# First norm and linear attention outputs of a decoder step: scaling in place and turning by the identity, instead of multiplying by a diagonal

## What is computed

```python
def rms_norm(x, w):
    y = x * rsqrt(mean(x * x, axis=-1) + EPS)
    return y * w

h = rms_norm(x, norm_mix_pre)               # x is (1024 + 8, 1024)
z = h @ w_in                                # projection to GLA q, k, v, r and NSA q, kv, gates
o, S = gla_chunked(q, k, v, g, s0)          # 4 heads of 128 output columns
o = o * rsqrt(mean(o * o, axis=-1) + EPS) * gla_norm
y_gla = o * silu(r)
y_nsa = compressed, selected and window attention, weighted by gates
x = x + rms_norm(concat(y_gla, y_nsa) @ w_out, norm_mix_post)
x = x + rms_norm(relu(rms_norm(x, norm_ffn_pre) @ w_ff_up)**2 @ w_ff_down, norm_ffn_post)
```

## Time and profile before

| | |
|---|---|
| median of three runs | 1752.52 us |
| the profiled execution, its time | 1760.71 us |
| its span in the trace | 1758.9 us |
| TensorE busy | 1684.2 us (96%) |
| VectorE busy | 1093.2 us (62%) |
| ScalarE busy | 518.2 us (29%) |
| GpSimd busy | 830.2 us (47%) |
| mean granted TensorE clock | 0.978 |

### The profile page before, as it was taken

How to read it: one execution, slowest core, us unless ns; L and a number is a source line. 1 busy time by engine, 2 the same in 40 slices (tenths; PEclk the granted TensorE clock), 3 DMA queues, 4 the chain that set the end, 5 groups by cost and what they waited for, 6 DMA issues and landing times.

```text
span 1758.9 us, 24643 instructions
## 1 busy us (share of the span) xinstructions
PE 1684.2 (96%) x9310; PEld 1369.3 (78%) x9310; DVE 1093.2 (62%) x2113; ACT 518.2 (29%) x1100; POOL 830.2 (47%) x644
## 2 busy tenths in 40 slices
PE   8999999897999989999999989999999999999997
PEld 7888888784555557777778878888888888888886
DVE  5332111446776667776641068896789678967897
ACT  3311111337887762334222162100120012001202
POOL 3211221314454452413222189957685668476933
PEclk9999999988999999999999999999999999999999
DMA  5488893838434545646643541121021201211005
GB/s 154 138 256 255 237 278 93 247 98 268 158 126 126 175 132 216 252 161 231 223 154 108 173 170 59 50 71 59 14 72 48 72 7 66 69 52 46 3 1 193
DMA packets 172396, 233.53 MB, mean 133 GB/s; under 512 B 22488, under 2 KB 137096, under 8 KB 168120
## 3 DMA queue, kind: packets, MB, share of 16 engines
q1 hardware_dynamic: 162024, 181.64, 33.6%
q0 software_dynamic: 9216, 50.34, 8.0%
q10 hardware_dynamic: 1040, 0.00, 0.0%
HBM read 217.58 MB, written 102.45 MB: 182 GB/s over the span
## 4 chain that ended last, share of the span: by engine, by line
PE 65%; DVE 6%; issue 2%; ACT 2%; POOL 2%; another core or an unknown queue 0%; DVEq 0%
PE PS L3137 36%; PE PS L2217 7%; PE PS L2415 6%; PE PS L1870 4%; PE PS L1855 4%; PE PS L1883 4%; DVE Z L2597 1%; DVE Z L3197 1%; POOL X L3071 1%; DVE Z L437 1%; PE PS L412 1%; POOL Z L1710 1%; PE PS L506 1%; PE PS L2261 0%; DVE Z L3157 0%
## 5 line engine op out<-in xcount | busy, mean ns | idle before, releaser
L3197 DVE TENSOR_TENSOR Z<-PS,Z 128x516 f32<-128x516 f32 x432 | 288.4, 686 | 118.8 <-PE PS L3137 117.5
L2217 PE MATMUL PS<-Z 128*128 128x256 f32 x768 | 189.4, 396 | 4.1 <-issue 3.2
L2217 PEld LDWEIGHTS PS<-Z 128*128 128x128 f32 x768 | 144.1, 196 | 33.4 <-issue 13.5
L3137 PE MATMUL PS<-Z,X 128*128 128x258 f32 x584 | 138.6, 384 | 2.6 <-POOL X L3071 2.6
L3137 PE MATMUL PS<-srow,misc 128*128 128x258 f32 x560 | 133.4, 381 | 0.0
L3137 PEld LDWEIGHTS PS<-Z,X 128*128 128x128 f32 x584 | 111.7, 192 | 19.9 <-POOL X L3071 3.0
L1144 DVE TENSOR_TENSOR Z<-PS,Z 128x516 f32<-128x516 f32 x27 | 18.8, 696 | 161.1 <-PE PS L312 161.1
L3137 PEld LDWEIGHTS PS<-srow,misc 128*128 128x128 f32 x560 | 106.0, 190 | 15.8
L3137 PE MATMUL PS<-srow,X 128*128 128x258 f32 x480 | 113.3, 380 | 0.0
L270 POOL TENSOR_TENSOR srow<-ring 128x512 f32<-128x512 f32 x15 | 21.2, 1410 | 194.0 <-PE PS L312 116.6
L3151 ACT ACTIVATE Z<-Z 128x2064 f32<-128x2064 f32 x16 | 30.8, 1924 | 248.2 <-DVE Z L3197 248.2
(11 more groups left out here) (484 smaller groups left out, 3827.7 us busy)
## 6 DMA issues: line engine op xcount, KB each, us to landing
packed_rows<-in_cache_nsa_kv SPq DMA_DIRECT2D x32, 1280.0 KB, 15.0
packed_blocks<-in_cache_nsa_kv SPq DMA_DIRECT2D x16, 2560.0 KB, 12.1
X<-in_w_ff_down SPq DMA_DIRECT2D x12, 1024.0 KB, 5.2
ring<-in_w_in SPq DMA_DIRECT2D x9, 1024.0 KB, 5.2
X<-in_x_prompt SPq DMA_DIRECT2D x8, 1024.0 KB, 13.1
ring<-in_w_ff_up SPq DMA_DIRECT2D x8, 1024.0 KB, 5.2
Z<-in_w_ff_up SPq DMA_DIRECT2D x8, 1024.0 KB, 5.2
out_y_prompt<-X SPq DMA_DIRECT2D x16, 512.0 KB
```

What stands on the lines that cost most here:

```text
L2217: last = nc.tensor.matmul(product(kind, v), w, x, start=(j == 0), stop=(j == 7))
L3137: last = nc.tensor.matmul(M.PS[:, N_.bank(n, e) + c, 0:HB], x[:, k, c * P:(c + 1) * P], y[:, k, :], start=e in (M1, M2, M5) and k == 0, st ...
L3197: nc.vector.tensor_tensor(N_.part(out, e), N_.view(n, e), N_.part(old, e), ALU.add).then_inc(N_.dve, 1)
```

## The change

The gain is loaded as eight rows of 128 numbers, turned by TensorE and copied to its old place by VectorE before its first use. Tile 0 and tile 1 of x are loaded by a DMA each. The diagonals of the first norm are gone: tiles 0, 2, 4 and 6 are scaled in place by VectorE directly after the reciprocal, tiles 1, 3, 5 and 7 by GpSimd, the 8 new tokens by ScalarE after all reciprocals; TensorE turns the scaled tile with eight transposes by the identity. In linear attention GpSimd scales `Osb` in place instead of making diagonals, and TensorE transposes. In the attention, for n = 0 and i = 0, the scores of unit 2 are issued before the turns. Some semaphores are named ahead of the block.

```diff
 def phase_load(nc, M, A, block):
+    M.gain_rows = M.Zf[0:KD, 9984:9984 + P]
+    first = M.sem_of_stage("first_x_loaded")
     @block.sync
     def _(sp):
-        load_x(sp, M, A)
+        rows = A["x_prompt"].rearrange("b (t p) d -> (b t) p d", p=P)
+        sp.dma_start(M.X[:, 0, :], rows[0]).then_inc(first, 16)
+        sp.dma_start(M.X[:, 1, :], rows[1]).then_inc(M.sem("x_loaded0"), 16)
+        load_x(sp, M, A, 1)
...
-        act.dma_start(M.nw[:, 0, :], A["norm_mix_pre"].rearrange("a (k p) -> p (a k)", p=P),
-                      allow_slow_non_contiguous=True).then_inc(M.sem("gain_loaded"), 16)
+        act.dma_start(M.gain_rows, A["norm_mix_pre"].rearrange("a (k p) -> (a k) p", p=P)).then_inc(M.sem("gain_loaded"), 16)
...
+        by_pool, by_act = (1, 3, 5, 7), (QT,)
+        by_dve = [i for i in range(NT) if i not in by_pool + by_act]
...
+        def turn_gain():
+            pe.wait_ge(M.sem("const_ready"), 3)
+            pe.wait_ge(M.sem("gain_loaded"), 16)
+            nc.tensor.transpose(M.PS[:, 6, 0:KD], M.gain_rows, M.ident[0:KD, 0:KD]).then_inc(gain_turned, 1)
+
+        def turn_scaled(i):
+            s, n = i % 2, toks(i)
+            wait_scaled(pe, i)
+            if i >= 2:
+                pe.wait_ge(evd, i - 1)
+            for k in range(KD):
+                last = nc.tensor.transpose(M.PS[:, 2 * s + k // 4, (k % 4) * P:(k % 4) * P + n],
+                                           x_tile(M, i)[:, k * P:(k + 1) * P], M.ident[0:n, 0:n])
+            last.then_inc(bkd, 1)
...
+        if use == 0:
+            act.wait_ge(norm.inverted, NT)
+            scaled(nc.scalar.activation(x_tile(M, QT), x_tile(M, QT), ACT.Copy, scale=st[0:B, 3, QT:QT + 1]), QT)
+
+    if use == 0:
+        @block.gpsimd
+        def _(pool):
+            for i in by_pool:
+                pool.wait_ge(norm.inverted, i + 1)
+                scaled(pool.tensor_scalar(x_tile(M, i), x_tile(M, i), st[:, 3, i:i + 1], None, ALU.mult), i)
...
             norm.invert(dve, i, 3)
-            if i >= 2:
-                dve.wait_ge(bkd, b0 + i - 1)
-            nc.vector.tensor_scalar(diag[0:n, i % 2, 0:n], M.ident[0:n, 0:n], r, None, ALU.mult).then_inc(dgr, 1)
+            if i in by_dve:
+                scaled(nc.vector.tensor_scalar(x_tile(M, i), x_tile(M, i), r, None, ALU.mult), i)
...
             if use == 0 and i == 0:
-                dve.wait_ge(M.sem("gain_loaded"), 16)
+                dve.wait_ge(gain_turned, 1)
+                nc.vector.tensor_copy(M.nw[:, 0, :], M.PS[:, 6, 0:KD]).then_inc(gain_turned, 1)
+                dve.wait_ge(gain_turned, 2)
...
-            def diagonals(t):
+            def scale_outputs(t):
                 pool.wait_ge(rsr, t + 1)
-                if t >= 2:
-                    pool.wait_ge(ybk, t - 1)
-                pool.tensor_tensor(dg[:, t % 2], M.ident[:, :].rearrange("p (j n) -> p j n", j=1).to_broadcast([P, GH, P]),
+                pool.tensor_tensor(Osb[:, t % 2], Osb[:, t % 2],
                                    root[:, t, :].rearrange("p (j n) -> p j n", n=1).to_broadcast([P, GH, P]), ALU.mult)\
-                    .then_inc(dgr, 1)
+                    .then_inc(scd, 1)
...
                 for j in range(GH):
-                    last = nc.tensor.matmul(M.PS[:, X + j // 2, 256 + j % 2 * P:256 + (j % 2 + 1) * P], Osb[:, t % 2, j, :], dg[:, t % 2, j, :],
-                                            start=True, stop=True)
+                    last = nc.tensor.transpose(M.PS[:, X + j // 2, 256 + j % 2 * P:256 + (j % 2 + 1) * P],
+                                               Osb[:, t % 2, j, :], M.ident[:, :])
...
             for i in range(J):
+                opening = n == 0 and i == 0
+                if opening:
+                    for c in share(2 * nchunk[n + 2], i, J):
+                        score(n + 2, c)
                 for j in pair(n, i):
                     turn(n, j)
                 for j in pair(n, i - 1):
                     values(n, j)
-                if n + 2 < NSU:
+                if n + 2 < NSU and not opening:
                     for c in share(2 * nchunk[n + 2], i, J):
                         score(n + 2, c)
```

More of the change, by code:

```diff
@@ L167, in _, with load_x @@
         dve.wait_ge(const, 3)
-def load_x(eng, M, A):
+def load_x(eng, M, A, first=0):
     xp = A["x_prompt"].rearrange("b (j t p) d -> (b j) p t d", t=2, p=P)
-    for j in range(QT // 2):
+    for j in range(first, QT // 2):
         eng.dma_start(M.X[:, 2 * j:2 * j + 2, :], xp[j]).then_inc(M.sem(f"x_loaded{j}"), 16)
@@ L455, in phase_norms, with scaled, wait_scaled @@
     rtb, invb, stored = M.sem("back_root"), M.sem("back_inverse"), M.sem("y_stored")
+    if use == 0:
+        gain_turned = M.sem_of_stage("gain_turned")
+        by_pool, by_act = (1, 3, 5, 7), (QT,)
+        by_dve = [i for i in range(NT) if i not in by_pool + by_act]
+        scaled_by = [(tiles, M.sem_of_stage(f"x_scaled_{name}"))
+                     for tiles, name in ((by_pool, "pool"), (by_act, "act"), (by_dve, "dve"))]
+    def scaled(ins, i):
+        for tiles, sem in scaled_by:
+            if i in tiles:
+                ins.then_inc(sem, 1)
+    def wait_scaled(eng, i):
+        for tiles, sem in scaled_by:
+            if i in tiles:
+                eng.wait_ge(sem, tiles.index(i) + 1)
     out = O["y_prompt"].rearrange("b (t p) d -> (b t) p d", p=P)
@@ L496, in _ @@
     def _(pe):
+        def turn_gain():
[11 more added lines that the diff above has]
+            last.then_inc(bkd, 1)
         def turn_back(i):
             s, n = i % 2, toks(i)
-            pe.wait_ge(dgr, b0 + i + 1)
+            pe.wait_ge(dgr, i + 1)
             if i == 0 and front is not None:
@@ L513, in _ @@
                 norm.turn(pe, i)
-            if back is not None and i >= PLAG:
+            if use == 0:
+                if i == 0:
+                    turn_gain()
+                turn_scaled(i)
+            elif back is not None and i >= PLAG:
                 turn_back(i - PLAG)
@@ L533, in square_back @@
             n = toks(i)
-            if front is None:
+            if i == 0 and front is None:
+                act.wait_ge(M.sem("first_x_loaded"), 16)
+            elif front is None:
                 wait_x(act, M, norm.order[i], 1)
@@ L1169, in phase_mid @@
     Osb = M.Zf[:, 23 * N:23 * N + 1024].rearrange("p (s j n) -> p s j n", s=2, j=GH)
-    dg = M.Zf[:, 22 * N:22 * N + 1024].rearrange("p (s j n) -> p s j n", s=2, j=GH)
     qs = M.misc[:, 2416:2432].rearrange("p (a b) -> p a b", a=2)
@@ L1182, in phase_mid @@
     orr, oev, sqr, ssr = T_("o_ready"), T_("o_moved"), T_("o_sq"), T_("o_ss")
-    rtr, rsr, dgr, ybk, fin = T_("o_root"), T_("o_scale"), T_("dg_ready"), T_("o_turned"), T_("o_mixed")
+    rtr, rsr, scd, ybk, fin = T_("o_root"), T_("o_scale"), T_("o_scaled"), T_("o_turned"), T_("o_mixed")
     stn, qsr, so, soe = T_("state_new"), T_("qs_ready"), T_("so_ready"), T_("so_moved")
@@ L1255, in _ @@
             for t in range(QT):
-                diagonals(t)
+                scale_outputs(t)
                 if t in (1, 2, 3):
@@ L1332, in turn_back @@
             def turn_back(t):
-                pe.wait_ge(dgr, t + 1)
+                pe.wait_ge(scd, t + 1)
                 pe.wait_ge(amr, min(t + 3, QT))
@@ L3506, in build @@
         for name in ("mix_summed", "rows_back", "out_weights_loaded", "new_rows_product", "new_rows_moved", "rows_loaded",
-                     "tail_on_scalar", "heads_joined"):
+                     "tail_on_scalar", "heads_joined", "blocks_gathered0", "blocks_gathered1", "blocks_gathered2",
+                     "blocks_gathered3", "new_row_placed0", "new_row_placed1", "new_rows_zeroed"):
             M.sem(name)
```

## The result

The changed kernel takes 1760.42 us, median of 6 runs (1758.96 to 1765.83), where the kernel before took 1753.36 on the same chip (6 runs, 1752.28 to 1754.61): the ratio is 1.004 with an interval of 1.003 to 1.005, so it is slower, by some 7 us. Forecast were 1755.9, with 1748.5 to 1760.5 as the range: the median lies 0.08 us under its upper end.

A forecast was written before the change was run, and what follows sets the result against it. TensorE, busy 96% of the span, was taken as the bound. Norm +5.2, projection's start +2.5, linear attention -2.5 and attention -1.8 gave +3.4 on the 1752.5 median: 1755.9 us, range 1748.5 to 1760.5.

The forecast's parts named there:

- linear attention's term: Linear attention: four fewer TensorE instructions per turn back shorten the loop and tail, -2.5 us, bounds -0.8 and -3.6.
- the norm's: First norm: last eviction ends at 33.1 instead of 27.86 at the lower clock level, +5.2 us.
- the other two: Projection's opening at the lower clock level, +2.5 us, and unit 2's scores moved ahead at the attention's start, -1.8 us.
- The serial round: First norm: odd tiles' GpSimd scaling, turn, eviction and reciprocal wait for each other, 6.4 us per two tiles.
- rival 1: First norm: TensorE runs at the upper clock level, norm +1.7, total -2.6 us, 1749.9; chance 20%.
- rival 2: First norm: GpSimd's four passes lengthen beside VectorE's scaling, 3.0 more, total +6.4 us, 1758.9; chance 13%.
- The lower level in the norm, and the projection's start behind it: TensorE stays at 1.2 GHz in the norm, and the projection's first 64 products start there: +2.5 us, bounds 0 and 2.8.
- Of six in the loop, 2.7 us, I take 1.6: Linear attention's loop: six shorter turns back save 2.7 us, of which 1.6 counts because later turns meet a wait.
- Half of the last turn: Linear attention's tail: the last turn back, 2.08 at the lower level, loses half its length, 0.9 us.
- Start of the attention: Unit 2's scores, moved ahead, fit into TensorE's pause for unit 0's weights: -1.8 us, bounds 0 and -3.34.
- step from the profiled execution to the median: Whole kernel: the profiled execution is 8.2 us above the 1752.5 median, and the summed difference carries over to it.
- the parts of the first eviction's start: First norm: load 4.4, square to reciprocal 1.5, scaling 0.75, turn 1.94, gain copy 0.4 put it near 9.2, not 12.03.

The follow-up runs named there:

- e4: The kernel before with all of the first norm's edit and nothing else: 1766.68 us, ratio 1.0051.
- e5: The changed kernel with VectorE's first-norm evictions queued one tile later: 1754.39 us, ratio 0.9998 to the kernel before.
- e7: The changed kernel with extra unread products keeping TensorE at work in the first norm: 1755.56 us, ratio 1.0011 to the kernel before.
- e1: The kernel before with the linear attention edit alone: 1760.35 us, ratio 1.0017.
- e13: e1 with nine extra unread products in linear attention's tail: 1760.35 us, ratio 1.0008 to the kernel before.
- e16: The whole change with all full-tile norm scaling on VectorE, 12 extra products before the first tile and e13's nine: 1755.35 us, ratio 0.9981 to the kernel before.
- e2: The kernel before with only unit 2's scores moved ahead of the first turns: 1757.14 us, ratio 0.999.
- e15: The kernel before with the loads part, 12 extra products before the first tile and the attention part, diagonals kept: 1752.01 us, ratio 0.9967.
- e14: The changed kernel with all full-tile norm scaling on VectorE, 12 extra products ahead, linear attention as before: 1755.16 us, ratio 0.998 to the kernel before.
- e3: The kernel before with only the loads changed (gain as rows and turned, tile 0 alone), diagonals kept: 1757.11 us, ratio 0.9991.

## Why the prediction came out as it did

Its direction and its account of the norm were right; the time was 4.5 us above the forecast, and that it fell inside the range is luck: three of the six executions lie above 1760.5, and the loss of 7.1 us is twice the 3.4 that were summed. Of the 4.5, 0.8 is the kernel before itself, which took 1753.36 beside the changed one and 1752.52 on record. The sum fell 4.8 short of the measured terms: linear attention's term had the wrong sign (4.3), the norm's was 1.1 too small, and the other two took 0.6 off again.

**The serial round: right, 1.1 us too short.** The last eviction ended at 34.2, forecast 33.1 (rival 1 had 29.6). GpSimd's first pass began 0.35 later, as tile 1's load landed later than was assumed (7.94 here, 7.52 to 7.72 in e4, e5 and e7). GpSimd's pass was put at 2.85 and took 2.86, 3.36, 3.36 and 2.84: +1.0 in all. The rest of a round, turn, eviction, reciprocal and handoffs, took 3.45 where the sum had 3.55, so three rounds gave 0.3 back, and the end took 0.1 more. The longer passes are what rival 2 foresaw, at a third of its price: it had four passes at +0.75, and it was two at +0.5, those beside which VectorE scaled a tile (15.97 in the rows above). That the scaling causes it isn't shown: in e5 and e7 it lies inside the pass too and costs 0.06 to 0.08. VectorE's scaling took the 0.75 that was estimated.

**The lower level in the norm, and the projection's start behind it: right.** Forecast 9.7 for the 64 products, measured 9.48 (8.58 in e4, which has the same norm); the main products started 2.3 later by it, forecast 2.5. This was stated from the earlier trace rows as a level that holds while TensorE works little, and e7 shows it from the other side: with work, the turn takes 1.09 and the 64 products 7.18.

**Linear attention: wrong, +1.8 in place of -2.5.** Two steps failed. "Of six in the loop, 2.7 us, I take 1.6": the loop gained 0.2 (from its start to the new tokens' products 52.5 us in place of 52.7), and over the executions without the slow opening it is 52.3 to 52.7 with the edit and 52.5 to 52.9 without. Each turn is 0.5 shorter, but TensorE then waits as much longer for others; in the rows above 0.83 for VectorE's L1564 and 1.07 for its L1530, where before the same two waits were 0.45 and 0.58. The loop was bound by that chain, as far as these waits show, and the 0.3 us between GpSimd's result and its use, which the prediction saw, was one sign of it. "Half of the last turn" was right in size: 2.08 became 1.11. What the sum lacked was that shorter turns leave TensorE idle, and that the 64 products of one column behind the pause would run at the lower level: 6.99 in place of 4.04, +2.95. That it belongs to this edit is shown by e1; that it is the idle time which brings the clock down rests on e13 and e16, where the extra products put off the fall and bring back 1.0 to 1.6 us. -0.2, -1.0 and +2.95 make the +1.8. The prediction charged this very mechanism for the norm and didn't ask for it in the second stage.

**Start of the attention: right.** -1.8 forecast, -2.2 in this pair, -2.4 in e2. Besides VectorE's wait of 1.32, the moved scores themselves ran 1.1 us shorter, at the upper level.

**The sum and what it was made against.** With the measured terms, 6.3 + 2.3 + 1.8 - 2.2 is +8.2, beside the +7.1 of the medians (5.3 to 8.8 by the ratio); the forecast's was +3.4. Its step from the profiled execution to the median was sound: the executions differ by up to 7.5 us in stretches that no edit touches, and the terms carried over to about 1 us. Three slips in the working change no term: the parts of the first eviction's start add up to 9.0 and not 9.2 (it started at 9.16), the last turn alone is 0.9 and not 0.8, and the lower level behind 404.8 lasted some 4.8 us (the granted clock is 0.72 from 409 to 410) and not 4.2, so that half of it is 2.4.

## What to carry to other kernels

Before an operation is moved to another engine, write out each engine's program order and look for a ring: here scaling on GpSimd, turn, eviction and the next reciprocal waited for each other, so an engine used for 3 us of every 6.8 set the pace of all. And where TensorE waits, the work that is taken from it may be what keeps its clock up: price what comes right behind at the lower level, and compare, as e15 does with e14, the kernel that keeps the cheap extra products.

## What the runs showed of the hardware that I had not expected

GpSimd's pass over 128x1024 takes 2.84 to 2.86 where VectorE only evicts beside it. With one VectorE scaling inside it it takes 3.36 twice in after and twice in e4, but 2.91 in e5 and 2.93 and 2.91 in e7, while VectorE's own took 0.75 each time. In the long ones the scaling begins 1.72 us behind the pass's start, in the short ones 1.27 to 1.29. What decides between 0.06 and 0.5 wasn't tried. Timeline of e5, which is to be held against the rows of after:

```profile
13.62 2.91 POOL L604 TENSOR_SCALAR X<-X,Z 128x1024 f32<-128x1024 f32 x1 [3.25 <-DVE Z L388]
...
14.89 0.75 DVE L628 TENSOR_SCALAR X<-X,Z 128x1024 f32<-128x1024 f32 x1
...
16.97 2.85 POOL L604 TENSOR_SCALAR X<-X,Z 128x1024 f32<-128x1024 f32 x1 [0.44 <-DVE Z L388]
```

The level of the clock in the opening of linear attention differs between executions whose code there is the same. In all of them the granted clock is 1.00 in the first 2 us of the stage, in which TensorE is busy 1.65 to 1.68. From 2 to 4 us behind the stage's start it is 0.53 or 0.54 in e3, e5 and e14, which stay at the lower level for some 10 us, 0.56 in e15, which is back at 1.00 less than 6 us behind the start, and 1.00 in the ten others. Stretches of before and then of e3, both from 2 us behind the start:

```profile
324.90:326.90 2.00, 2.00 (x32) 1.49 (x32) 1.20 (x5) 0.05 (x1) 2.00 (x2) 1.00 1.07 354
```

```profile
321.30:323.30 2.00, 2.00 (x26) 1.34 (x25) 0.61 (x3) 0.00 (x0) 2.00 (x2) 0.54 1.07 358
```

Up to the new tokens' products it costs 3.6 to 4.0 us in those three and 0.6 in e15. What decides it stays open.
